# A float32 transformer on one core: the forget gate's selection as 16 columns with stride zero, the latents split straight from PSUM, the rotary key put into the heads' keys by two transfers

## The reference

```python
# block 2: FoX attention, 16 heads of 64
log_f = log_sigmoid(f_logit); cum = cumsum(log_f)
s = q @ k.T * scale + (cum[t] - cum[s])        # decay bias per head
# block 3: latent attention (MLA)
a    = rmsnorm(h, kv_norm) @ w_kv_a            # 256 latents and 32 rotary columns
c_kv = rmsnorm(a[..., :256], ckv_norm)
k_rope = rope(a[..., 256:], positions)         # one rotary key for all 16 heads
k = concat([c_kv @ w_uk, broadcast(k_rope)]);  v = c_kv @ w_uv
c_q = rmsnorm(rmsnorm(h, attn_norm) @ w_dq, cq_norm)   # 768 latents
q = c_q @ w_uq                                 # 16 heads of 64 and 32 rotary columns
# y = rmsnorm(x): x * rsqrt(mean(x * x) + 1e-6) * gain
```

## Time and profile before

| | |
|---|---|
| runs | 1046.95 us (1046.88 to 1050.2) |
| profiled execution | 1046.38 us |
| its span, first to last instruction | 1044.7 us |
| PE, DVE, ACT, POOL busy | 97%, 64%, 54%, 7% |
| mean granted TensorE clock | 0.995 |
| DMA engines | 49.4% for the slabs and outputs |

### The profile page before, as it was taken

How to read it: one execution, slowest core, us unless ns; L and a number is a source line. 1 busy time by engine, 2 the same in 40 slices (tenths; PEclk the granted TensorE clock), 3 DMA queues, 4 the chain that set the end, 5 groups by cost and what they waited for, 6 DMA issues and landing times.

```text
span 1044.7 us, 21989 instructions
## 1 busy us (share of the span) xinstructions
PE 1017.8 (97%) x8296; PEld 990.4 (95%) x8296; DVE 671.3 (64%) x1221; ACT 561.9 (54%) x949; POOL 74.5 (7%) x84
## 2 busy tenths in 40 slices
PE   6999999989999999999999999999899999999997
PEld 6999899989999999999999999999799899999996
DVE  5545988776565658666576565658877675555554
ACT  6566786544444446565564444448576664444443
POOL 2021000140000001000010000003400010000000
PEclk9999999999999999999999999999999999999999
DMA  8644345455555555434455555554543345656531
GB/s 331 219 135 142 121 142 162 141 165 184 186 181 182 187 179 163 143 122 143 141 179 183 181 184 178 187 175 150 173 142 122 122 135 193 193 175 195 172 122 41
DMA packets 48152, 171.71 MB, mean 164 GB/s; under 512 B 5344, under 2 KB 6624, under 8 KB 47968
## 3 DMA queue, kind: packets, MB, share of 16 engines
q1 hardware_dynamic: 48096, 170.93, 49.4%
HBM read 169.86 MB, written 1.05 MB: 164 GB/s over the span
## 4 chain that ended last, share of the span: by engine, by line
PE 88%; DVE 7%; ACT 2%; issue 1%; DMA 1%; SPq 0%; POOLq 0%; POOL 0%; ACTq 0%; DVEq 0%
PE bank L310 87%; DVE w_lo L1137 2%; DVE a_lo L1149 2%; PE bank L500 1%; DVE xT L1166 1%; DVE arena L1130 1%; ACT w_hi L790 1%; DVE arena_r L1149 1%; DMA stage<-slab_dram 1%; DVE tmp L1130 1%; ACT a_hi L825 0%; ACT L971 0%; DVE arena L1396 0%; ACT soft_p L875 0%; SPq L276 0%
## 5 line engine op out<-in xcount | busy, mean ns | idle before, releaser
L790 ACT ACTIVATE w_hi<-stage 128x1024 fp32r<-128x1024 f32 x319 | 334.1, 1052 | 188.3 <-PE bank L310 184.3
L310 PE MATMUL bank<-a_hi,w_hi 128*128 128x256 f32 x1488 | 425.5, 287 | 9.7 <-ACT a_hi L985 7.3
L310 PE MATMUL bank<-a_hi,w_lo 128*128 128x256 f32 x1488 | 419.9, 283 | 0.0
L310 PE MATMUL bank<-a_lo,w_hi 128*128 128x256 f32 x1488 | 414.8, 283 | 0.0
L1137 DVE TENSOR_TENSOR w_lo<-stage,w_hi 128x1024 fp32r<-128x1024 f32 x319 | 391.5, 1244 | 11.0 <-ACT w_hi L790 10.7
L310 PE MATMUL bank<-arena_r,w_hi 128*128 128x256 f32 x1840 | 339.8, 286 | 7.7 <-DVE arena_r L1137 3.9
L310 PEld LDWEIGHTS bank<-a_hi,w_hi 128*128 128x128 f32 x1488 | 286.1, 192 | 14.0 <-DVE w_lo L1137 9.6
L310 PEld LDWEIGHTS bank<-arena_r,w_hi 128*128 128x128 f32 x1840 | 289.1, 193 | 9.8 <-DVE arena_r L1137 4.8
L310 PEld LDWEIGHTS bank<-a_hi,w_lo 128*128 128x128 f32 x1488 | 286.1, 192 | 0.0
L310 PEld LDWEIGHTS bank<-a_lo,w_hi 128*128 128x128 f32 x1488 | 283.1, 192 | 1.3 <-issue 1.2
L310 PE MATMUL bank<-arena_r,w_lo 128*128 128x256 f32 x920 | 260.6, 284 | 0.0
(11 more groups left out here) (152 smaller groups left out, 745.7 us busy)
## 6 DMA issues: line engine op xcount, KB each, us to landing
stage<-slab_dram SPq DMA_DIRECT2D x319, 512.0 KB, 3.5
con<-con_dram SPq DMA_DIRECT2D x1, 1153.5 KB, 11.9
xT<-xT_dram SPq DMA_DIRECT2D x4, 256.0 KB, 5.8
out_dram<-arena SPq DMA_DIRECT2D x8, 128.0 KB, 2.0
vec<-vec_dram SPq DMA_DIRECT2D x1, 245.5 KB, 3.8
pos<-pos_dram SPq DMA_DIRECT2D x1, 128.0 KB, 11.7
```

Source lines behind the costliest of these rows:

```text
L310: return nc.tensor.matmul(out, lhsT, rhs, start=start, stop=True, skip_group_check=True)
L790: nc.scalar.activation(w_hi[:, slot, :], stage[:, slot, :], ACT.Copy).then_inc(hi_made, 1)
```

## The change

Three edits, and a fourth that follows from the second.

`pick` becomes a tensor of its own with 16 columns, one for each head, and the weights are one column repeated 128 times by a stride of zero. The latents lose their product with `rB`: ACT takes high part and square, DVE the low part, straight from the bank, so the bank is free only when the low part is made. Since the latents then lack the factor `rB`, the eps of their norm is scaled: `eps_v` is eps x (mean + eps) of the residual's own norm, DVE makes it and the sum of mean square and `eps_v` (`mean_square`), and ACT's two steps follow (`inverse_root`). DVE makes all eight low parts of the key/value input. And the rotary key goes to the heads by two transfers on ACT's queue, each of 32 partitions x 16 heads x 256 values, 512 KB.

```diff
-        cq, ckv = chunks(arena, 8192, 6), chunks(arena, 8192 + 1536, 2)
+        eps_v = span(arena, 8192, TOK)
-        pick = span(arena_r, 4096, 2048).rearrange("p (h t) -> p h t", t=P)
+        pick = sb("pick", [P, HEADS], f32r)
...
 # PE
-                        pe.wait_ge(*((blo_ready, k + 1) if k < 5 else (plo_ready, k - 4)))
+                        pe.wait_ge(blo_ready, k + 1)
...
-                        last = mm(b[:, out], pick[r, g, :], decay[r, of_k], False)
+                        last = mm(b[:, out], pick[r, g:g + 1].to_broadcast([48, P]), decay[r, of_k], False)
...
-                pe.wait_ge(krope_ready, h // 8 + 1)
-                pe.wait_ge(krope2_ready, h // 8 + 1)
+                pe.wait_ge(krope_ready, 32)
...
                 if i >= 4:
-                    pe.wait_ge(lat_raw, i - 3)
+                    pe.wait_ge(latlo_ready, i - 3)
...
 # ACT
+            def inverse_root(t):
+                chain(nc.scalar.activation(t, t, ACT.Ln))
+                return nc.scalar.activation(t, t, ACT.Exp, scale=-0.5)
...
-                raw, g, hi, _ = latent(i)
-                act.wait_ge(lat_raw, i + 1)
-                nc.scalar.activation(hi, raw, ACT.Copy, scale=g).then_inc(lathi_ready, 1)
+                raw, (g, hi, _) = lat_bank(i), latent(i)
+                act.wait_ge(slab_done, DQ + i + 1)
...
+                nc.scalar.activation(hi, raw, ACT.Copy, scale=g).then_inc(lathi_ready, 1)
...
-                nc.scalar.activation(mla_k[96:128, 8 * i:8 * i + 8, :], half_heads(k_rope[64:96, :]), ACT.Copy
-                                     ).then_inc(krope2_ready, 1)
+                for r in (64, 96):
+                    nc.scalar.dma_start(mla_k[r:r + 32, :, :],
+                                        k_rope[64:96, :].unsqueeze(1).to_broadcast([32, HEADS, TOK])
+                                        ).then_inc(krope_ready, 16)
...
 # DVE
+            def key_value_low(c):
+                dve.wait_ge(bhi_ready, c + 1)
+                scaled_lo(b_lo[:, c, :], xT[:, c, :], gain(7, c), b_hi[:, c, :]).then_inc(blo_ready, 1)
+
+            def mean_square(out, count):
+                nc.vector.scalar_tensor_tensor(out, half(7, 0), 1.0 / count, eps_v, ALU.mult, ALU.add
+                                               ).then_inc(latms_ready, 1)
...
+                next_lo(n)
+                for c in {1: (0, 1), 2: (2, 3), 3: (4,), 4: (5,), 5: (6, 7)}.get(i, ()):
+                    key_value_low(c)
...
-                        times(raw, lat_bank(j), rB[:, :]).then_inc(lat_raw, 1)
...
-                        scaled_lo(lo, raw, g, hi).then_inc(latlo_ready, 1)
+                    scaled_lo(lo, lat_bank(j), g, hi).then_inc(latlo_ready, 1)
...
 # POOL
-                    nc.gpsimd.memset(pick[:, :, :].bitcast(f32), 0.0).then_inc(pick_clear, 1)
+                    nc.gpsimd.memset(pick[:, :].bitcast(f32), 0.0).then_inc(pick_clear, 1)
...
-                        nc.gpsimd.tensor_copy(
-                            pick[a:a + 16, :, :], ident[a:a + 16, a:a + 16].unsqueeze(2).to_broadcast([16, 16, P])
-                        ).then_inc(pick_ready, 1)
+                        nc.gpsimd.tensor_copy(pick[a:a + 16, :], ident[a:a + 16, a:a + 16]).then_inc(pick_ready, 1)
...
-            for i in range(5):
-                add_squares(add_index(5) - 6 + i, 1, 6)
-                if i < 3:
-                    kv_low(5 + i)
+            add_squares(add_index(5) - 6, 5, 6)
             add_squares(add_index(5) - 1, 1, 7)
-            pool.wait_ge(rope_ready, 1)
-            pool.wait_ge(sq_added, add_index(5))
-            for i in range(2):
-                nc.gpsimd.tensor_copy(mla_k[64:96, 8 * i:8 * i + 8, :], half_heads(k_rope[64:96, :])
-                                      ).then_inc(krope_ready, 1)
-                pool.wait_ge(krope_ready, i + 1)
```

More of the change, by code:

```diff
@@ L167, in trunk @@
         x_ready, ahi_ready, alo_ready = sem("x_ready"), sem("ahi_ready"), sem("alo_ready")
-        bhi_ready, b_scaled, blo_ready, plo_ready = (sem(n) for n in ("bhi_ready", "b_scaled", "blo_ready", "plo_ready"))
+        bhi_ready, blo_ready = sem("bhi_ready"), sem("blo_ready")
         sum_done, r_ready, col_done, col_ready = sem("sum_done"), sem("r_ready"), sem("col_done"), sem("col_ready")
@@ L209, in latent @@
             if i < 6:
-                return cq[:, i, :], span(vec, V_CQ + i, 1), cq_hi[:, i, :], cq_lo[:, i, :]
-            return ckv[:, i - 6, :], span(vec, V_CKV + i - 6, 1), ckv_hi[:, i - 6, :], ckv_lo[:, i - 6, :]
+                return span(vec, V_CQ + i, 1), cq_hi[:, i, :], cq_lo[:, i, :]
+            return span(vec, V_CKV + i - 6, 1), ckv_hi[:, i - 6, :], ckv_lo[:, i - 6, :]
         def lat_bank(i):
@@ L254, in uq_out @@
             return half((4, 0, 1, 2)[h % 4], 0)
-        def half_heads(x):
-            return x.unsqueeze(1).to_broadcast([x.shape[0], HEADS // 2, TOK])
         def add_index(m):
@@ L1075, in _ @@
                     latent_split(1)
-                if i == 7:
-                    inverse_rms(rQ[:, :], half(7, 0), 768).then_inc(latr_ready, 1)
                 if 2 <= i < 8:
@@ L1080, in _, with rope_keys @@
                 next_hi(n)
[L1081 removed]
+                if i == 7:
+                    act.wait_ge(latms_ready, 1)
+                    inverse_root(rQ[:, :]).then_inc(latr_ready, 1)
+            def rope_keys():
                 act.wait_ge(rope_ready, 1)
[L1084 to L1085 removed]
+                for r in (64, 96):
+                    nc.scalar.dma_start(mla_k[r:r + 32, :, :],
+                                        k_rope[64:96, :].unsqueeze(1).to_broadcast([32, HEADS, TOK])
+                                        ).then_inc(krope_ready, 16)
             for e in range(4):
                 if e == 1:
[L1090 to L1091 removed]
+                    act.wait_ge(latms_ready, 2)
+                    inverse_root(rKV[:, :]).then_inc(latr_ready, 1)
                 if e >= 2:
@@ L1100, in _ @@
                 if e == 1:
-                    rope_keys(0)
+                    rope_keys()
             for s in range(12):
@@ L1495, in _ @@
-                if 1 <= i < 6:
-                    dve.wait_ge(bhi_ready, i)
-                    scaled_lo(b_lo[:, i - 1, :], xT[:, i - 1, :], gain(7, i - 1), b_hi[:, i - 1, :]
-                              ).then_inc(blo_ready, 1)
-                for j in {0: (), 1: (0, 1)}.get(i, (i,)):
-                    dve.wait_ge(slab_done, DQ + j + 1)
-                    dve.wait_ge(r_ready, 5)
-                    if j < 8:
-                        raw, g, hi, lo = latent(j)
-                        times(raw, lat_bank(j), rB[:, :]).then_inc(lat_raw, 1)
-                        if j:
-                            next_lo(n)
-                        dve.wait_ge(lathi_ready, j + 1)
-                        scaled_lo(lo, raw, g, hi).then_inc(latlo_ready, 1)
-                    else:
-                        b = lat_bank(8)
-                        times(k_rope[64:96, :], b[64:96, :], trig[64:96, :])
-                        chain(times(tmp[64:96, 0, :], b[96:128, :], trig[96:128, :]))
-                        chain(nc.vector.tensor_tensor(k_rope[64:96, :], k_rope[64:96, :], tmp[64:96, 0, :], ALU.add))
-                        times(k_rope[64:96, :], k_rope[64:96, :], rB[64:96, :]).then_inc(rope_ready, 1)
@@ L1516, in _ @@
-                if i == 7:
+                next_lo(n)
+                for c in {1: (0, 1), 2: (2, 3), 3: (4,), 4: (5,), 5: (6, 7)}.get(i, ()):
+                    key_value_low(c)
+                if i == 2:
+                    dve.wait_ge(sum_done, 5)
+                    nc.vector.tensor_scalar(eps_v, half(7, 0), EPS / D, EPS * EPS, ALU.mult, ALU.add
+                                            ).then_inc(epsv_ready, 1)
+                for j in {0: (), 1: (0, 1), 8: ()}.get(i, (i,)):
+                    g, hi, lo = latent(j)
+                    dve.wait_ge(lathi_ready, j + 1)
+                    scaled_lo(lo, lat_bank(j), g, hi).then_inc(latlo_ready, 1)
@@ new lines, in _ @@
+                if i == 7:
+                    dve.wait_ge(latsum_done, 1)
+                    dve.wait_ge(epsv_ready, 1)
+                    mean_square(rQ[:, :], 768)
+                if i == 8:
+                    b = lat_bank(8)
+                    dve.wait_ge(slab_done, n + 1)
+                    dve.wait_ge(r_ready, 5)
+                    times(k_rope[64:96, :], b[64:96, :], trig[64:96, :])
+                    chain(times(tmp[64:96, 0, :], b[96:128, :], trig[96:128, :]))
+                    chain(nc.vector.tensor_tensor(k_rope[64:96, :], k_rope[64:96, :], tmp[64:96, 0, :], ALU.add))
+                    times(k_rope[64:96, :], k_rope[64:96, :], rB[64:96, :]).then_inc(rope_ready, 1)
@@ L1524, in _ @@
                 if e == 1:
+                    dve.wait_ge(latsum_done, 2)
+                    mean_square(rKV[:, :], 256)
                     dve.wait_ge(latr_ready, 2)
```

27 lines of the change are left out of this document (5 added, 22 removed).

## The result

The changed kernel takes 1036.1 us (median of 4 runs, 1035.6 to 1036.3), the kernel before 1046.9 us in the same comparison: ratio 0.989, 95% interval 0.987 to 0.991. A second comparison of the same two kernels gave 1037.9 us (1036.2 to 1038.1) against 1046.7, ratio 0.991 (0.989 to 0.992). The forecast was 1036.0 with a range of 1034.3 to 1040.5. The profiled execution took 1035.6 us for a span of 1033.9.

The account below looks back on a forecast made before the run. TensorE, busy 97%, was taken as the bound, with time to win from waits for VectorE's low parts and low clock: 5.3 + 5.7 = 11.0 us off 1046.4 gives 1035.4, median 0.6 above, so 1036.0; range 1034.3 to 1040.5.

Parts of the forecast that it names:

- First FFN, 5.3 us: Start of first FFN: smaller selection frees VectorE; of 5.6 us lost to wait and low clock, 0.3 stays, gain 5.3.
- Weights with stride zero, 0: FoX scores: 32 weight loads of one column with stride zero cost 0, at most 6.0 us.
- Latents, 5.7 us: Latents' slabs to keys: TensorE's waits for VectorE and the low clock, 6.0 us, go but for 0.3; gain 5.7.
- the rest: Latents' slabs: TensorE's remaining wait for VectorE's low parts, taken as 0.3 us (0 to 1.3).
- The keys' round: Keys' mean square, VectorE to ScalarE and back: first key products end at 749.7, before TensorE's need; 0.5 us wait goes.
- Transfers, 0: Rotary key: two transfers land in 7 us, before the last attention's first score; cost 0, bounds 0 and 0.8 us.
- A: Last attention's scores: the rotary key's transfers land late and TensorE waits; 1036.8 to 1042.0, middle 1039 us; chance 0.14.
- B: FoX scores: stride-zero weights can't load beside a matmul; up to 6.0 us, middle 1039 us; chance 0.06.
- C: Latents' stage: low parts stay at 0.84 us beside GpSimd's additions; 2.6 us wait plus 1.5 clock, 1040 us; chance 0.06.
- D: Rotary key's transfers bound by number of pieces: 28 us, TensorE stands 16.5 us; 1054.0 us, slower; chance 0.04.
- E: First FFN: additions and small casts still hold VectorE, so only 5.7 us come off; 1041.3 us; chance 0.04.

Follow-up runs that it names:

- e1_pick: The kernel before with the selection alone changed (16 columns, weights with stride zero, small fill): 1041.6 us, ratio 0.995.
- e4_stride: The kernel before with its full table, only the score matmuls reading one column with stride zero as weights: 1047.0 us, ratio 1.000.
- e3_copies: The changed kernel with the rotary key put into the heads' keys by GpSimd's and ScalarE's copies instead of the two transfers: 1042.1 us, ratio 0.995.
- e2_latents: The kernel before with the latents' part alone changed, without the selection and the transfers: 1046.3 us, ratio 1.000.
- e7_later: The changed kernel with the two transfers issued one slab later on ScalarE's queue: 1037.0 us, ratio 0.991.
- e6_copies_late: As e3_copies, with GpSimd's two copies held back until ScalarE has written the keys' inverse root: 1036.1 us, ratio 0.990.
- e5_spread: The changed kernel with the forget gate's 32 small products spread over the next slab of values: 1034.6 us, ratio 0.988.

## Why the prediction came out right, and where it was not

*First FFN, 5.3 us.* This is right: 5.47 in the profile, 5.3 by e1_pick. The four splits take 5.17 us as at the second FFN, and no wait is left where 0.3 was allowed.

*Weights with stride zero, 0.* This is right, as e4_stride shows.

*Latents, 5.7 us.* The number is right, 5.58 from the latents to the values; its account is not. Of the steps, the low parts from 718.55 to 730.2 take 11.7 us for the predicted 11.75. They began later than reckoned, so the rest was 0.69 for 0.3, and the clock did stay up. The keys' round came 1.2 us later than predicted (the first key products end at 745.8, which is 750.9 on the scale of before, for 749.7), but PE too was 0.9 later, and the 0.5 us went.

*Transfers, 0.* This step fails. Time of issue (748.4 for 748.6, on the scale of before) and need (760.2 for 760.1) came as worked out, and nothing waits for them. The landing did not: reckoned at 756 it came at 758.7, so that 1.5 us of slack were left of 4. And above all, the worth of the part lies in the copies that it removes. The working used 2.3 us for the two splits ahead of the keys' mean square, "no longer" 4.05, and booked that under the latents. (The 2.3 follows from the three splits of the earlier trace rows; the earlier trace rows has only the 4.05.) The splits are only short because POOL's copies go. e3_copies shows 6 us for it in the profile, 4 to 6 in the medians, and e2_latents that the latents' part alone brings 0.6. By the medians, one part put on top of another, the selection takes off 5.3 us, the latents' part adds 0.5, and the transfers take off 4 to 6. The whole came out right because the change holds both parts. The profile of before had both facts, a 4.05 us row where 2.3 stands undisturbed and a copy beside it; asked for each part alone, they would have pointed to this.

*Rivals.* A (late transfers) is out, but only by 1.5 us in one profile and 2.7 in the other, and e7_later shows 0.7 us of loss for 3.6 of delay. B (weights with stride zero) is out. C (DVE stays the bound) holds in small: DVE's rows beside POOL's additions do take 0.96 for 0.47, but only a few, and PE waits 0.69 us, not 2.6. D (bound by pieces) is out: 10.2 us from first issue to last completion, where pieces at a slab's price would take 28. E (no effect) is out: the small casts take 1.05 us each and still don't hold DVE.

*What no case had.* The gate's low clock cost 1.5 us here and 3 in other executions, and the start was 1.15 us shorter by scatter. The two nearly cancelled (0.4 us), so that 1036.0 fits to 0.1 us is luck; the second comparison stood 1.9 us above it. The prediction had looked for a low clock only behind some 4 us of idle PE; the gate's came with no wait in the row.

The Trainium skill, page "SBUF — State Buffer" (Door 1: the DMA port swizzle), gave an estimated 5.5 us for both transfers alone. They took 10.2 us from the first issue to the last completion, 9.1 in the second profile, beside slab loads with the DMA engines full (share 1.0 from 746 us to 752). The warning had the right sign and did not decide. No run here has the transfers alone.

## What to carry to other kernels

Price each part of a change alone before summing: where a new step is put behind rows of an engine, ask what stretches these rows today, and whether the same change removes it. The same two copies on GpSimd cost nothing, 1.3 us or 6 us by which VectorE rows they meet and what waits behind these; moving their start by one wait was as good as replacing them. A row of small matmuls can be followed by a low clock with no wait in it; here it helped to put them between large ones.

## What the runs showed of the hardware

GpSimd and VectorE. A split with both inputs in SBUF goes from 1.2 to 2.8 us beside GpSimd's copies of 32 x 2048 (e3_copies, 5.63 us for two, the mean of a pair), while key products with one input in PSUM take 2.79 us for four beside such a copy (e6_copies_late) as without (the changed kernel). The Trainium skill, page "SBUF — State Buffer" (Who interferes with whom), says that among the engines only the port pair of VectorE and GpSimd contends, and that a VectorE operation with two SBUF inputs and a GpSimd operation that reads SBUF exclude each other. The traces agree with it: 2.8 against 1.2 us with two inputs in SBUF, no difference with one. What they add: four casts of 16 x 16 beside four splits left these at 5.17 us, though each shows 1.05 us, so a GpSimd row's length is not the time for which it stops VectorE.

The clock. It fell during or just behind the row of 32 products of 32 columns in eight of eleven profiles, with no wait of PE in the row, and stayed low for 3.4 to 6.8 us at 0.21 us a step for 0.12. Spread among products of 256 columns it fell there in none of three. That is few profiles; the gain of e5_spread, all at this place, points the same way. The Trainium skill, page "TensorE: Matmul & The Clock Gate" (Part 1), says that how many slow matmuls one kernel shows at its start varies from run to run. The traces agree and show it in the middle of a kernel too: the two profiles of the changed kernel have 3.4 and 6.8 us of low clock at the gate.
